# A transformer block on one core: VectorE takes row maxima ahead of a rotary tile, and the sums of modulation accumulators stand as a block behind a tile

## The chip, the core and the metric

The kernel runs on one core of a Trainium2 chip. The metric is the device time of one execution in microseconds. A core has five engines that run their own instruction streams and wait for each other on semaphores: TensorE (PE, matmuls), VectorE (DVE), ScalarE (ACT), GpSimd (POOL) and SyncE (SP, which here issues nearly all DMAs). Matmuls write to PSUM, eight banks of 128 x 512 float32.

## What is computed

One block of a hybrid network over 512 tokens of width 1024, in float32:

```
mod = silu(c) @ ada_w + ada_b
shift1, scale1, gate1, shift2, scale2, gate2 = split(mod, 6)
h = rmsnorm(x, norm1_w) * (1 + scale1) + shift1
gq, gk, gv, gr, g_lr, aq, ak, av, merge_a, merge_b = split(h @ w_in)
y_gla = (rmsnorm(gla_chunked(gq, gk, gv, log_sigmoid(g_lr @ w2 + b) / 16)) * silu(gr)) @ w_gla_branch
y_attn = dilated_attention(rotary(aq), rotary(ak), av) @ w_attn_branch
x = x + gate1 * ((sigmoid(merge_a) * y_gla + sigmoid(merge_b) * y_attn) @ w_out)
h2 = rmsnorm(x, norm2_w) * (1 + scale2) + shift2
x = x + gate2 * (causal_conv_ffn_hidden(h2, w_up, conv_w, conv_b) @ w_down)
out = rmsnorm(x, final_norm_w)
```

`dilated_attention` has three groups of four heads (dilations 1, 4, 16); each softmax needs the maximum of each row of scores. The `mod` vector is 6144 numbers, from a matrix of 25 MB.

## The kernel before

**Products.** Weights arrive in *units* of 1 MB or less (`UNITS`, line 90): ("v", ..), ("qk", p, g) for the query and key columns of head pair p and group g, ("lr", ..) for 16 columns of low rank, then ("gqk", h), ("gv", h), ("gr", h) for the four heads of the gated recurrence, and so on. Each unit gives one or two *tiles* (`tiles_of`), each 128 x 512 in PSUM. To keep float32 precision a weight is split into a high part (ScalarE, `split_hi`) and a rest (VectorE, `split_lo`), and so is h; a tile is 8 steps of k with 3 matmuls each (`three`, lines 1485 to 1487), 24 matmuls.

**Banks.** `TILES` lists all tiles in order; tile i lies in `bank[i % 2]`. `take(i)` (line 1515) waits on TensorE until the tile two places ahead has been read out and its bank is free (`acc_free`). Who reads it out depends on the kind: for "qk" VectorE in `rotate(j, t)` (L1054, L1055), j = 3p + g. The other six banks (`side`) are for attention and the recurrence.

**Modulation.** The last four parts of `mod` (gate1, shift2, scale2, gate2) are not made by TensorE alone. SP loads 16 chunks of 1 MB of `ada_w` between the units (`RAW`), two buffers taking turns. For each VectorE does `modulate(n)` (L1016 or L1018): multiply by a scalar per partition and add to `ada_acc`, 128 x 2048. After 8 chunks (r = 0 after n = 7, r = 1 after n = 15) TensorE sums over the partitions: 16 float32 matmuls of 128 columns of `ada_acc` against one column of ones (L1582), into the tile ("ada", r). VectorE adds the bias in `ada_tile(r)` (L1033), which frees that bank.

`WITH_ADA` names the two tiles that carry these sums: ("qk", 1, 2), 1 and ("gr", 2, 0), 1. In `TILES` the tile ("ada", r) stands ahead of the tile that carries it, and `product` puts three of the sums behind each k of that tile (`ada_part`).

**Attention for a pair of heads** (p = 0 beside the units ("qk", 1, g)) goes in steps `attention(p, i)`, written out on each engine: i = 0, 1 scores (TensorE), mask and maxima (VectorE); i = 2 TensorE transposes the maxima (L1662, L1664), VectorE takes the row maxima of both heads (L1109, L1111); i = 3 TensorE transposes them back (L1669, L1672), VectorE makes `negm` (L1116), ScalarE the exponentials (L643); i = 4 TensorE transposes (L1621), ScalarE and VectorE copy to PT (L656, L1125); i = 5, 6 the values. TensorE does a step between two tiles.

**Rotary.** `rotate` leaves products with cosine and sine in `rope` and `rope_t`; GpSimd adds the halves (L534) when both tiles of the unit are there. `rotate(j, 0)` waits for GpSimd to be through with j - 1 (`rope_sum`), as `rope_t` is used again. SP then issues eight shuffles to `qk` (L424) and the next weights; a load waits until its buffer has been used (`raw_used`, which VectorE counts up in `split_lo` and `modulate`).

The order on every engine is written out by hand: the engines' loops over p, g and t.

Of the kernel before, what the change touches and what calls it, by code (L numbers as in the profile page):

```python
# [19 lines left out]
KT = D // P  # L20
# [7 lines left out]
GROUPS = 3  # L28
# [80 lines left out]

WITH_ADA = {(("qk", 1, 2), 1): 0, (("gr", 2, 0), 1): 1}
TILES = []
for _u in UNITS:
    for _t in range(tiles_of(_u)):
        if (_u, _t) in WITH_ADA:
            TILES += [("ada", WITH_ADA[_u, _t])]
        TILES += [(_u, _t)]
    if _u == ("gqk", 0, 0):
        TILES += [("z", b) for b in range(NB)]  # L120
TILE = {t: n for n, t in enumerate(TILES)}
# [9 lines left out]
RAW_AT = {r: q for q, r in enumerate(RAW)}  # L131
# [19 lines left out]
def hybrid_block_kernel(nc, x, c, positions, ada_w, ada_b, norm1_w, w_in, gate_w2, gate_b, gla_norm_w,  # L151
# [3 lines left out]
    with ctx:  # L155
# [93 lines left out]
        bank = [ctx.enter_context(nc.psum_tensor(f"bank{i}", [P, SEQ], F32)) for i in range(8)]  # L249
# [4 lines left out]
        raw_used = sem("raw_used")  # L254
        hi_done = sem("hi_done")
        acc_ready = sem("acc_ready")
# [680 lines left out]
        def _(dve):  # L937
# [361 lines left out]
            for p in range(2):  # L1299
                for g in range(GROUPS):  # L1300
                    n = UNIT[("qk", p, g)]
                    if p == 0 or g == 0:
                        rotate(GROUPS * p + g, 0)
                        split_lo(n + 1)
                        rotate(GROUPS * p + g, 1)
                        modulate(n)
                        if p == 1:
                            attention(0, 0)
                    else:
                        split_lo(n + 1)  # L1310
                        if g == 1:
                            attention(0, 1)
                            rotate(GROUPS + g, 0)
                            modulate(n)
                        else:
                            rotate(GROUPS + g, 0)
                            attention(0, 3)
                            ada_tile(0)
                        rotate(GROUPS + g, 1)
                        if g == 2:  # L1320
                            modulate(n)
                        attention(0, 2 * g)
            n = UNIT[("lr", 0, 0)]
            split_lo(n + 1)
            modulate(n)
# [2 lines left out]
            for h in range(HEADS):  # L1328
                for u, kind in enumerate(("gqk", "gv", "gr")):
                    n = UNIT[(kind, h, 0)]  # L1330
# [24 lines left out]
            for u in range(4):  # L1355
                split_lo(UNIT[("ma", u, 0)] + 1)
                for t in range(2):
                    i = 2 * u + t
# [120 lines left out]
        def _(pe):  # L1479
# [35 lines left out]
            def take(i):  # L1515

                if i >= 2:
                    pe.wait_ge(acc_free[i % 2], i // 2)
                return bank[i % 2]

            def product(n, t):

                kind, a, _ = UNITS[n]
                slot = n % 2
                i = TILE[(UNITS[n], t)]
                ada = WITH_ADA.get((UNITS[n], t))
                if ada is not None:
                    take(i - 1)
                    pe.wait_ge(raw_used, RAW_AT[("ada", KT * (ada + 1) - 1)] + 1)
                dst = take(i)  # L1530
                if t == 0:
                    pe.wait_ge(raw_used, RAW_AT[("w", n)] + 1)
                if kind in ("v", "gv"):
                    for half in range(2):
                        blk = 2 * t + half
                        tok = slice(blk * P, (blk + 1) * P)
                        for k in range(KT):
                            w = tuple(v[:, slot, k * UW:(k + 1) * UW] for v in (w_hi, w_lo))
                            s = tuple(v[:, k, tok] for v in (h_hi, h_lo))
                            last = three(dst[:, half * UW:(half + 1) * UW], s, w, k == 0, k == KT - 1)  # L1540
                else:
                    if kind == "wa":
                        nk, width, at, src = 2, D, t * P, (oa_hi, oa_lo)
                    elif kind == "lr":
                        nk, width, at, src = KT, LOWRANK, 0, (h_hi, h_lo)
                    else:
                        nk, width, at = KT, UW, t * P
                        src = {"wg": (og_hi, og_lo), "wo": (mix_hi, mix_lo)}.get(kind, (h_hi, h_lo))
                    m = LOWRANK if kind == "lr" else P
                    if kind == "wa" and t == 0:  # L1550
                        pe.wait_ge(oalo_done, 2)
                    if kind == "wg" and a == 0 and t == 0:
                        pe.wait_ge(oglo_done, HEADS)
                    for k in range(nk):
                        if kind == "wo" and a == 0 and t == 0:
                            pe.wait_ge(mixlo_done, k + 1)
                        w = tuple(v[:, slot, k * width + at:k * width + at + m] for v in (w_hi, w_lo))
                        last = three(dst[0:m, :], w, tuple(v[:, k, :] for v in src), k == 0, k == nk - 1)
                        if ada is not None and k < nk - 1:
                            ada_part(ada, k)  # L1560
                last.then_inc(acc_ready, 1)

            def wide_values(half):
# [11 lines left out]
                if half == 0:  # L1575
                    last.then_inc(vw_half, 1)

            def ada_part(r, k):

                dst = bank[TILE[("ada", r)] % 2]  # L1580
                for j in range(3 * k, min(3 * k + 3, 2 * KT)):
                    last = pe.matmul(dst[:, j:j + 1], ada_acc[:, j * P:(j + 1) * P], ones[:, 0:1],  # L1582
                                     start=(j == 0), stop=True, skip_group_check=True)
                    if j == 2 * KT - 1:
                        last.then_inc(acc_ready, 1)

            def scores(hh, banks=range(4)):
                p, hd = divmod(hh, 2)
# [208 lines left out]
            for p in range(2):  # L1797
                for g in range(GROUPS):
                    for t in range(2):
                        product(UNIT[("qk", p, g)], t)  # L1800
                        if p == 1 and 2 * g + t > 0:
                            attention(0, 2 * g + t - 1)
            product(UNIT[("lr", 0, 0)], 0)
            attention(0, 5)

            for h in range(HEADS):
                for u, kind in enumerate(("gqk", "gv", "gr")):
                    for t in range(2):
                        i = 2 * u + t
                        product(UNIT[(kind, h, 0)], t)  # L1810
                        if h == 0 and i == 0:
                            attention(0, 6)
                        if h == 0:
                            attention(1, i)
                        if h == 1 and i == 0:
                            attention(1, 6)
                        if h >= 2 and i in (0, 2, 3):
                            gla(h - 2, 6 + i)
                        if h >= 1:
                            gla(h - 1, i)  # L1820
                    if h == 0 and kind == "gqk":
                        gate_tiles()

# [142 lines left out]
```

## Time and profile before

| | |
|---|---|
| median of 3 runs | 983.17 us (982.35 to 984.64) |
| profiled execution | 981.5 us, span of its core 979.7 us |
| TensorE busy, share of the span | 95% |
| VectorE | 53% |
| ScalarE | 38% |
| GpSimd | 10% |
| mean granted TensorE clock | 0.97 of full speed |
| read from HBM, written | 104.77 MB, 4.19 MB |
| chain of work that ended last: TensorE's share | 87% |

The span is the time from the first to the last instruction of the profiled execution. Matmul rows of the timeline carry a start and a duration; matmuls are pipelined, so durations overlap and the time that a run of them takes is read from start to start. The profiler records each float32 matmul of the sums as two (32 records for 16 matmuls). "Clock 1.00" in these rows is 2.4 GHz, 0.50 is 1.2 GHz.

### The profile page before, as it was taken

What the parts mean: (1) busy time and instruction counts of PE and PEld (TensorE: products, weight loads), DVE (VectorE), ACT (ScalarE), POOL (GpSimd) and SP (SyncE); (2) the same over time, 40 slices, a digit from 0 to 9 for tenths busy, and PEclk for the clock granted to TensorE, in tenths of its full rate; (3) what the DMA queues carried; (4) which work ended last, traced back from release to release, by engine and by line L of the source; (5) the groups of instructions that cost most, each with busy time, mean ns of one, the idle gap of its engine ahead of it and who ended that gap; (6) DMA issues with size and microseconds to landing.
All of it is one profiled execution on the core that took longest, in us unless ns stands there. A gap on an engine that the chain in (4) does not pass through costs nothing.

```text
span 979.7 us, 11999 instructions
## 1 busy us (share of the span) xinstructions
PE 931.3 (95%) x4659; PEld 782.5 (80%) x4659; DVE 522.8 (53%) x643; ACT 373.0 (38%) x457; POOL 94.6 (10%) x66
## 2 busy tenths in 40 slices
PE   2689998999999999999999997999999999999996
PEld 2589887779988988888888885888888888888885
DVE  5994774565574646463254436655555555523323
ACT  5362111547634334544322323433433344332225
POOL 4720421100000000000002222000000000000003
PEclk8699997989999999999999999999999999999998
DMA  9926764424351212122222441234333432322302
GB/s 323 355 90 190 213 186 121 151 87 140 118 173 50 80 43 87 45 85 86 86 87 86 172 129 54 75 98 116 86 86 100 114 86 86 114 102 86 120 9 86
DMA packets 114015, 112.68 MB, mean 115 GB/s; under 512 B 4516, under 2 KB 104230, under 8 KB 111671
## 3 DMA queue, kind: packets, MB, share of 16 engines
q1 hardware_dynamic: 113255, 109.96, 35.6%
q10 hardware_dynamic: 720, 2.16, 0.6%
q8 instruction: 28, 0.46, 0.2%
q14 instruction: 12, 0.10, 0.0%
HBM read 104.77 MB, written 4.19 MB: 111 GB/s over the span
## 4 chain that ended last, share of the span: by engine, by line
PE 87%; DVE 7%; issue 2%; DMA 1%; POOL 1%; SPq 1%; ACT 1%; DVEq 0%; ACTq 0%; POOLq 0%
PE bank L1485 25%; PE bank L1486 25%; PE bank L1487 25%; DVE ada_in L959 2%; PE bank L1700 2%; POOL rope L534 1%; DMA ada_in<-in_ada_w_dram 1%; PE bank L1582 1%; PE bank L1879 1%; PE bank L1721 1%; PE bank L1646 1%; DVE w_lo L993 1%; PE bank L1621 1%; DVE h_lo L1413 1%; DVE rope_t L1055 1%
## 5 line engine op out<-in xcount | busy, mean ns | idle before, releaser
L1485 PE MATMUL bank<-h_hi,w_hi 128*128 128x512 f32 (+1 forms) x696 | 278.7, 400 | 3.6 <-DVE rope_t L1055 2.6
L1487 PE MATMUL bank<-h_hi,w_lo 128*128 128x512 f32 (+1 forms) x696 | 273.0, 392 | 0.0
L1486 PE MATMUL bank<-h_lo,w_hi 128*128 128x512 f32 (+1 forms) x696 | 272.9, 392 | 0.0
L1485 PEld LDWEIGHTS bank<-h_hi,w_hi 128*128 128x128 f32 (+1 forms) x696 | 131.2, 188 | 32.2 <-issue 3.5
L1487 PEld LDWEIGHTS bank<-h_hi,w_lo 128*128 128x128 f32 (+1 forms) x696 | 131.0, 188 | 28.9
L1486 PEld LDWEIGHTS bank<-h_lo,w_hi 128*128 128x128 f32 (+1 forms) x696 | 131.2, 189 | 26.9 <-issue 0.2
L993 DVE TENSOR_TENSOR w_lo<-raw,w_hi 128x2048 fp32r<-128x2048 f32 (+3 forms) x48 | 88.2, 1848 | 61.8 <-ACT w_hi L566 61.8
L1000 DVE TENSOR_TENSOR w_lo<-raw,w_hi 128x2048 fp32r<-128x2048 f32 x32 | 73.4, 2293 | 88.8 <-ACT w_hi L574 88.8
L566 ACT ACTIVATE w_hi<-raw 128x2048 fp32r<-128x2048 f32 (+2 forms) x45 | 73.4, 1644 | 73.1 <-DMA raw<-in_w_in_dram 64.5
L1439 DVE SCALAR_TENSOR_TENSOR conv<-bank,vecs,conv 128x511 f32<-128x511 f32 x88 | 65.7, 748 | 66.5 <-ACT conv L888 61.0
L574 ACT ACTIVATE w_hi<-raw 128x2048 fp32r<-128x2048 f32 x33 | 62.9, 1905 | 69.3 <-PE bank L1487 69.3
L888 ACT ACTIVATE conv<-bank,vecs 128x512 f32<-128x512 f32 x44 | 34.1, 778 | 105.6 <-PE bank L1487 105.0
L1485 PE MATMUL bank<-hs_hi,w_hi 128*128 128x512 f32 x176 | 68.6, 390 | 0.0
L1487 PE MATMUL bank<-hs_hi,w_lo 128*128 128x512 f32 x176 | 68.5, 389 | 0.0
L1486 PE MATMUL bank<-hs_lo,w_hi 128*128 128x512 f32 x176 | 68.5, 389 | 0.0
L1485 PE MATMUL bank<-w_hi,h_hi 128*128 128x256 f32 (+1 forms) x160 | 50.5, 316 | 0.0
L1486 PE MATMUL bank<-w_lo,h_hi 128*128 128x256 f32 (+1 forms) x160 | 49.8, 311 | 0.0
L1487 PE MATMUL bank<-w_hi,h_lo 128*128 128x256 f32 (+1 forms) x160 | 49.8, 311 | 0.0
L1487 PEld LDWEIGHTS bank<-hs_hi,w_lo 128*128 128x128 f32 x176 | 33.0, 188 | 6.9
L1486 PEld LDWEIGHTS bank<-hs_lo,w_hi 128*128 128x128 f32 x176 | 33.0, 188 | 6.9
L1485 PEld LDWEIGHTS bank<-hs_hi,w_hi 128*128 128x128 f32 x176 | 33.0, 188 | 6.7
L506 POOL COPY sq_sum<-sq 128x512 f32<-128x512 f32 x3 | 1.8, 610 | 366.9 <-ACT sq L581 366.9
(235 smaller groups left out, 1340.1 us busy)
## 6 DMA issues: line engine op xcount, KB each, us to landing
raw<-in_w_up_dram SPq DMA_DIRECT2D x44, 512.0 KB, 4.5
raw<-in_w_in_dram SPq DMA_DIRECT2D x19, 1024.0 KB, 5.2
raw<-in_ada_w_dram SPq DMA_DIRECT2D x16, 1024.0 KB, 5.5
raw<-in_w_down_dram SPq DMA_DIRECT2D x22, 512.0 KB, 3.9
raw<-in_w_in_dram SPq DMA_DIRECT2D x20, 512.0 KB, 5.1
ada_in<-in_ada_w_dram SPq DMA_DIRECT2D x16, 512.0 KB, 8.9
raw<-in_w_gla_branch_dram SPq DMA_DIRECT2D x4, 1024.0 KB, 5.0
raw<-in_w_out_dram SPq DMA_DIRECT2D x4, 1024.0 KB, 5.3
```

What stands on the lines that cost most here:

```text
L534: pool.tensor_tensor(dst, dst, rope_t[:, half, :], op).then_inc(rope_sum, 1)
L566: last = act.activation(hv, r, ACT.Copy)
L574: act.activation(w_hi[:, slot, :], raw[:, slot, :], ACT.Copy).then_inc(hi_done, 1)
L888: act.activation(conv[:, s, t, :], bank[2 * s + t][:, :], ACT.Identity, scale=vecs[:, bass.ds(i + (V_CW2 + t * FT), 1)], bias=vecs[:, bass ...
L959: dve.scalar_tensor_tensor(total, ada_rows(j, k), c_silu[:, k:k + 1], total, ALU.mult, ALU.add).then_inc(ada_step, 1)
L993: last = dve.tensor_tensor(lv, r, hv.bitcast(F32), ALU.subtract)
L1000: dve.tensor_tensor(w_lo[:, slot, :], raw[:, slot, :], w_hi[:, slot, :].bitcast(F32), ALU.subtract).then_inc(raw_used, 1)
L1439: ins = dve.scalar_tensor_tensor(conv[:, s, t, tap:SEQ], src[:, 0:SEQ - tap], vecs[:, bass.ds(i + (col + t * FT), 1)], conv[:, s, t, tap:S ...
L1485: pe.matmul(out_ap, wh, xh, start=first, stop=False, skip_group_check=True)
L1486: pe.matmul(out_ap, wh, xl, start=False, stop=False, skip_group_check=True)
L1487: return pe.matmul(out_ap, wl, xh, start=False, stop=last, skip_group_check=True)
L1700: pe.matmul(side[2][0:m, at:at + CHUNK], kk[:, n, 0:m], q_in[:, h % 2, b * P + at:b * P + at + CHUNK], start=True, stop=True, skip_group_c ...
```

## The change

The table of tiles that carry sums becomes one of tiles that are followed by them; ("ada", r) moves behind its tile in `TILES`. TensorE no longer mixes the sums in: `modulation_sums(r)` issues all 16 in one block, the first after the tile ("qk", 1, 2), 1 and `attention(0, 4)`, ahead of ("lr", 0, 0); the second after ("gr", 2, 0), 1 and the recurrence's steps behind it, ahead of ("gqk", 3, 0). On VectorE the steps beside ("qk", 1, 1) and ("qk", 1, 2) stand in another order.

```diff
-WITH_ADA = {(("qk", 1, 2), 1): 0, (("gr", 2, 0), 1): 1}
+AFTER_TILE = {(("qk", 1, 2), 1): 0, (("gr", 2, 0), 1): 1}
 TILES = []
 for _u in UNITS:
     for _t in range(tiles_of(_u)):
-        if (_u, _t) in WITH_ADA:
-            TILES += [("ada", WITH_ADA[_u, _t])]
         TILES += [(_u, _t)]
+        if (_u, _t) in AFTER_TILE:
+            TILES += [("ada", AFTER_TILE[_u, _t])]
...
                         if p == 1:
                             attention(0, 0)
+                    elif g == 1:
+                        split_lo(n + 1)
+                        attention(0, 1)
+                        rotate(GROUPS + g, 0)
+                        attention(0, 2)
+                        rotate(GROUPS + g, 1)
+                        modulate(n)
                     else:
+                        rotate(GROUPS + g, 0)
+                        attention(0, 3)
                         split_lo(n + 1)
-                        if g == 1:
-                            attention(0, 1)
-                            rotate(GROUPS + g, 0)
-                            modulate(n)
-                        else:
-                            rotate(GROUPS + g, 0)
-                            attention(0, 3)
-                            ada_tile(0)
                         rotate(GROUPS + g, 1)
-                        if g == 2:
-                            modulate(n)
-                        attention(0, 2 * g)
+                        ada_tile(0)
+                        modulate(n)
+                        attention(0, 4)
...
                 i = TILE[(UNITS[n], t)]
-                ada = WITH_ADA.get((UNITS[n], t))
-                if ada is not None:
-                    take(i - 1)
-                    pe.wait_ge(raw_used, RAW_AT[("ada", KT * (ada + 1) - 1)] + 1)
                 dst = take(i)
...
                         last = three(dst[0:m, :], w, tuple(v[:, k, :] for v in src), k == 0, k == nk - 1)
-                        if ada is not None and k < nk - 1:
-                            ada_part(ada, k)
...
-            def ada_part(r, k):
-
-                dst = bank[TILE[("ada", r)] % 2]
-                for j in range(3 * k, min(3 * k + 3, 2 * KT)):
+            def modulation_sums(r):
+
+                dst = take(TILE[("ada", r)])
+                pe.wait_ge(raw_used, RAW_AT[("ada", KT * (r + 1) - 1)] + 1)
+                for j in range(2 * KT):
                     last = pe.matmul(dst[:, j:j + 1], ada_acc[:, j * P:(j + 1) * P], ones[:, 0:1],
                                      start=(j == 0), stop=True, skip_group_check=True)
-                    if j == 2 * KT - 1:
-                        last.then_inc(acc_ready, 1)
+                last.then_inc(acc_ready, 1)
...
+            modulation_sums(0)
             product(UNIT[("lr", 0, 0)], 0)
...
+                        if (kind, h, t) == ("gr", 2, 1):
+                            modulation_sums(1)
```

How this moves the instructions at two places. TensorE before, from the end of the tile ("qk", 1, 2), 0 (in `bank0`) on: the transposes of `attention(0, 3)`, then the next tile with its sums.

```order
L1487 MATMUL bank0<-h_hi,w_lo 128x512
L1669 MATMUL bank2<-cst,rowm 128x2 x4
L1672 MATMUL bank2<-cst,rowm 128x2 x4
L1485 MATMUL bank0<-h_hi,w_hi 128x512
L1486 MATMUL bank0<-h_lo,w_hi 128x512
L1487 MATMUL bank0<-h_hi,w_lo 128x512
L1582 MATMUL bank1<-ones,ada_acc 128x1 x3
L1485 MATMUL bank0<-h_hi,w_hi 128x512
```

TensorE with the change, at the same place:

```order
L1488 MATMUL bank0<-h_hi,w_lo 128x512
L1664 MATMUL bank2<-cst,rowm 128x2 x4
L1667 MATMUL bank2<-cst,rowm 128x2 x4
L1486 MATMUL bank1<-h_hi,w_hi 128x512
L1487 MATMUL bank1<-h_lo,w_hi 128x512
L1488 MATMUL bank1<-h_hi,w_lo 128x512
L1486 MATMUL bank1<-h_hi,w_hi 128x512
```

The tile is now in `bank1` and has no sums in it. TensorE with the change, from that tile's end on: the transposes of `attention(0, 4)`, the sums, the 16-column tile "lr".

```order
L1488 MATMUL bank1<-h_hi,w_lo 128x512
L1616 MATMUL bank2<-cst,S 128x128 x4
L1616 MATMUL bank3<-cst,S 128x128 x3
L1616 MATMUL bank4<-cst,S 128x128 x4
L1616 MATMUL bank5<-cst,S 128x128 x4
L1578 MATMUL bank0<-ones,ada_acc 128x1 x16
L1486 MATMUL bank1<-h_hi,w_hi 16x512
```

The sums stand in one row of 16, in `bank0`. VectorE beside ("qk", 1, 1), as a difference, from the end of `rotate(4, 0)` to `rotate(5, 0)` (L1054 and L1055 are a rotation, L1018 a part of the modulation, `rowm` the row maxima):

```order
 L1055 TENSOR_TENSOR rope_t<-bank0,cs 128x512
-L1018 SCALAR_TENSOR_TENSOR ada_acc<-raw,c_silu,ada_acc 128x2048
+L1109 COPY rowm<-bank2 2x512
+L1111 TENSOR_TENSOR rowm<-bank3,rowm 2x512
 L1054 TENSOR_TENSOR rope<-bank1,cs 128x512
 L1055 TENSOR_TENSOR rope_t<-bank1,cs 128x512
-L1109 COPY rowm<-bank2 2x512
-L1111 TENSOR_TENSOR rowm<-bank3,rowm 2x512
-L993 TENSOR_TENSOR w_lo<-raw,w_hi 128x128
+L1018 SCALAR_TENSOR_TENSOR ada_acc<-raw,c_silu,ada_acc 128x2048
 L1054 TENSOR_TENSOR rope<-bank0,cs 128x512
 L1055 TENSOR_TENSOR rope_t<-bank0,cs 128x512
```

The row maxima moved ahead of `rotate(4, 1)`, the modulation behind it. The same difference goes on, from `negm` to the first modulation part of r = 1:

```order
 L1116 TENSOR_SCALAR negm<-bank2 128x16
-L1033 TENSOR_TENSOR mod<-bank1,vecs 128x16
-L1054 TENSOR_TENSOR rope<-bank0,cs 128x512
-L1055 TENSOR_TENSOR rope_t<-bank0,cs 128x512
+L993 TENSOR_TENSOR w_lo<-raw,w_hi 128x128
+L1054 TENSOR_TENSOR rope<-bank1,cs 128x512
+L1055 TENSOR_TENSOR rope_t<-bank1,cs 128x512
+L1033 TENSOR_TENSOR mod<-bank0,vecs 128x16
 L1016 TENSOR_SCALAR ada_acc<-raw,c_silu 128x2048
```

`ada_tile(0)` (L1033) now stands behind `rotate(5, 1)`, and the small `split_lo` between the two rotations.

## Rows read from the trace of the kernel before

**Rows 1.** The page, part 2: granted clock of TensorE in 40 equal slices, in tenths.
```profile
PEclk8699997989999999999999999999999999999998
```

**Rows 2.** Stretches: length, each engine's busy time (x instructions), granted clock, DMA, GB/s.
```profile
159.00:176.00 17.00, 17.00 (x56) 14.79 (x57) 0.17 (x1) 3.90 (x12) 0.00 (x0) 0.50 0.33 86
176.10:188.20 12.10, 12.10 (x84) 8.87 (x83) 9.16 (x8) 8.07 (x19) 3.92 (x3) 1.00 0.43 132
213.70:220.30 6.60, 6.60 (x22) 4.50 (x21) 0.00 (x0) 5.22 (x11) 0.00 (x0) 0.50 0.00 0
336.00:344.00 8.00, 8.00 (x54) 7.14 (x52) 2.51 (x10) 1.02 (x1) 0.00 (x0) 1.00 0.34 117
599.20:602.60 3.40, 0.38 (x2) 0.37 (x3) 1.91 (x3) 2.35 (x5) 0.00 (x0) 1.00 0.00 0
602.70:606.00 3.30, 3.30 (x9) 2.56 (x9) 3.09 (x5) 3.17 (x4) 1.32 (x1) 0.50 0.01 2
607.70:610.20 2.50, 0.01 (x1) 0.00 (x0) 2.50 (x1) 0.00 (x0) 1.95 (x1) 1.00 0.00 0
```

**Rows 3.** TensorE's timeline, 148 to 189 us: start, duration, instructions [idle before, releaser].
```profile
148.77 0.60 PE L1662 MATMUL bank<-cst,mx 128*2 128x128 f32 x4
...
159.00 0.77 PE L1485 MATMUL bank<-h_hi,w_hi 128*128 128x512 f32 x1 [2.48 <-DVE rope_t L1055]
...
176.14 1.80 PE L1621 MATMUL bank<-cst,S 128*128 128x128 f32 x15
...
188.24 0.48 PE L1485 MATMUL bank<-h_hi,w_hi 128*128 128x512 f32 x1
```

**Rows 4.** VectorE's timeline, 149 to 181 us.
```profile
149.83 2.35 DVE L1018 SCALAR_TENSOR_TENSOR ada_acc<-raw,c_silu,ada_acc 128x2048 f32<-128x2048 f32 x1
152.09 1.05 DVE L1054 TENSOR_TENSOR rope<-bank,cs 128x512 f32<-128x512 f32 x1
...
154.02 0.67 DVE L1109 COPY rowm<-bank 2x512 f32<-2x512 f32 x1
...
156.85 1.05 DVE L1054 TENSOR_TENSOR rope<-bank,cs 128x512 f32<-128x512 f32 x1 [1.16 <-POOL rope L534]
...
178.36 1.27 DVE L1016 TENSOR_SCALAR ada_acc<-raw,c_silu 128x2048 f32<-128x2048 f32 x1
179.55 1.28 DVE L1125 COPY PT<-bank 128x512 f32<-128x512 f32 x2
```

**Rows 5.** GpSimd's timeline at 154 us.
```profile
154.25 2.56 POOL L534 TENSOR_TENSOR rope<-rope,rope_t 128x512 f32<-128x512 f32 x2 [18.29 <-DVE rope_t L1055]
```

**Rows 6.** ScalarE's timeline: exponentials of the first head; later, split of (gqk, 0, 0).
```profile
158.97 3.93 ACT L643 ACTIVATE S<-S,negm 128x256 f32<-128x256 f32 x12 [7.91 <-DVE negm L1116]
...
181.48 1.90 ACT L566 ACTIVATE w_hi<-raw 128x2048 fp32r<-128x2048 f32 x1
```

**Rows 7.** SP's timeline: the first chunk of r = 1, and the weights of (gqk, 0, 0).
```profile
152.21 0.35 SPq L389 DMA_DIRECT2D raw<-in_ada_w_dram  x1
...
162.48 0.58 SPq L398 DMA_DIRECT2D raw<-in_w_in_dram  x1
```

**Rows 8.** Chain that ended last: start, time on the chain, three sums at either clock.
```profile
160.62 1.07 PE bank L1582 x6
...
337.12 0.56 PE bank L1582 x6
```

**Rows 9.** TensorE's timeline, 327 to 350 us, around the tile (gr, 2, 0), 1.
```profile
327.67 0.58 PE L1485 MATMUL bank<-h_hi,w_hi 128*128 128x512 f32 x1
...
333.43 1.52 PE L1700 MATMUL bank<-q_in,kk 128*32 128x16 f32 x16
...
336.09 0.58 PE L1485 MATMUL bank<-h_hi,w_hi 128*128 128x512 f32 x1
...
345.52 1.52 PE L1700 MATMUL bank<-q_in,kk 128*32 128x16 f32 x16
...
349.19 0.50 PE L1485 MATMUL bank<-h_hi,w_hi 128*128 128x512 f32 x1 [0.66 <-DVE mod L1033]
```

## The prediction

> **What bounds the kernel now.** Begin with the page. TensorE is the engine that is busy nearly always, so a kernel like this gets shorter in two ways: TensorE waits less, or it works less time at the half clock. The line of the granted clock reads 9 or 10 tenths except in a few slices; the seventh of the 40 (147 to 171 us) shows 7 [rows 1]. The second view is the table of stretches: from 159.0 to 176.0 us TensorE is busy throughout at clock 0.50 (1.2 GHz), and from 176.1 on it is at 1.00 (2.4 GHz) [rows 2].
>
> TensorE's own timeline says what stands there [rows 3]. Before the tile (qk, 1, 2), 1 it idles 2.48 us, from 156.5 to 159.0, released by VectorE's L1055. This is the wait for the PSUM bank: tiles alternate between two banks, the accumulator tile "ada" 0 holds bank 1, so the tile needs bank 0, which `rotate(5, 0)` frees. VectorE's timeline shows that this rotation starts at 156.85, behind GpSimd, which adds the halves of the previous rotary pair until 154.25 + 2.56 = 156.81 and could begin only after VectorE's late rotation of that pair [rows 4, 5]. Then the tile, with the sums between its matmuls, takes 176.14 - 159.00 = 17.14 us. A tile of the same 24 matmuls alone takes 333.43 - 327.67 = 5.76 us at the full clock [rows 9].
>
> What the engine did around the moves of its clock: it had transposed a few columns and then idled when the clock fell; while one-column matmuls stood between the 512-column ones the clock stayed at 0.50 for 17 us; with the plain matmuls that end the tile it came back. At 336 to 344 us the same mixture runs at clock 1.00 [rows 2]: it does not bring the clock down, but from 0.50 it has not brought it up.
>
> **The change, part by part.** (1) The tile moves to the other bank: it takes bank 1, freed by `rotate(4, 1)` at about 153.2 (below). TensorE is done with the step before at 156.5. The wait of **2.48 us** goes. What is late next there: the transposes behind the tile need ScalarE's exponentials, see (3).
>
> (2) The sums stand behind the tile instead of inside. Six passes (three fp32 matmuls) take 0.56 us at clock 1.00 and 1.07 us at 0.50 [rows 8]. The 16 matmuls are 32 passes: 32/6 x 0.56 = 2.99 us, or 5.7 at the half clock. No row has such a block; these two bound it, and I take 2.99, as the block follows dense work at full clock. First place: 17.14 - 5.76 - 2.99 = **8.39 us** less. Second place: 349.19 - 336.09 = 13.10 us now; then a tile alone, 5.76, the steps of the recurrence behind it, 349.19 - 0.66 - 345.52 = 3.01, and the block, 2.99. So **1.34 us** goes, in it the 0.66 us that the next tile waited for VectorE's `ada_tile(1)`, since the bank it takes is then another [rows 9].
> A pass at full clock is 93 ns by the row, and 178 ns at the half clock. By the Trainium skill (TensorE: Matmul & The Clock Gate, LDWEIGHTS) a weight load costs its columns over 1.2: an estimate of 107 ns a pass, 3.4 us a block, and a gain that is smaller by 0.9 us over both. The row here is shorter and follows the clock; it decides.
>
> (3) VectorE's order. Nothing is added; steps change places. `attention(0, 2)` (two instructions, 0.67 us for the first) now precedes `rotate(4, 1)`. Its input is TensorE's transposes, which begin at 148.77, 1.1 us before VectorE turns to it at 149.83 [rows 3]: a few tenths of wait at most. `rotate(4, 1)` starts about 151.3 instead of 152.09, and the 2.35 us of modulation go behind it, to 155.5. GpSimd's 2.56 us then end at 156.0, `rotate(5, 0)` starts there, 0.85 us sooner than now, and so do `negm` and the exponentials behind it, which now start at 158.97 and take 3.93 us [rows 4 to 6]. They would end near 162.1. The moved tile ends at 156.5 + 5.76 = 162.3, and the last exponentials are wanted about a microsecond into the transposes. So this order saves 0 by itself, as cover: without it the margin would be some 0.5 us.
> `ada_tile(0)` and what is behind it on VectorE (`modulate(8)` and two copies to PT, 178.36 to 180.83 in the trace, 2.5 us) wait for the block's end: 162.3 + 1.8 of transposes [rows 3] + 3.0 = 167.1. They are done by 169.6. TensorE wants PT after the "lr" tile, another 24 matmuls, at 172.9. Hidden with 3 us to spare.
> SP's queue: `modulate(7)` ends 3.3 us later, so the load behind it is issued at 155.5 instead of 152.21. The eight shuffles behind wait for GpSimd as before, a little earlier, and the weights of (gqk, 0, 0) follow near 161.6 instead of 162.48 [rows 7]. Their split on ScalarE starts at 181.48 with no idle before it [rows 6]: it waits for the engine, not for a landing. With the exponentials of the second head through near 168, both halves are split by about 172. TensorE reaches them at 188.24 - 2.48 - 8.39 = 177.4: hidden with 5 us to spare.
>
> **The sum.** 2.48 + 8.39 + 1.34 = 12.2 us, if the clock stays up. Against this stands the clock in the new blocks: 3.0 us of one-column matmuls resemble the idle stretches. Of these, 599.2 to 602.6 brought the clock down and 607.7 to 610.2 did not [rows 2]. Between these ends I take one fall over the two blocks, with the shortest low stretch of the trace, 3.3 us (602.7 to 606.0), which costs half of itself, 1.65. So 12.2 - 1.65 = 10.6 us.
> The sum is against the profiled execution, 981.5 us (span 979.7), which is 1.67 us under the median of the runs, 983.17. The stretch that goes is one whose length varies with when the clock returns, so some of these 1.67 us may go too; I take half. 983.17 - 0.8 - 10.6 = **971.8 us**.
>
> **Rivals.** (A) No fall at all: 971.8 - 1.65 = 970.2. For it: the mixture at 336 to 344 held the clock, and 2.5 us of nothing did. (B) Both blocks bring it down and for long, as the 6.6 us at 213.7 to 220.3 [rows 2]: 3.3 us each, 970.2 + 6.6 = 976.8. For it: the first block follows 1.8 us of transposes, and if those are quiet too it is 4.8 us.
> The Trainium skill (the same page, Part 4: PE-mode transpose) says that transposes do not count as busy work for the clock. By it case B gains at the first block; no row here tests it alone.
> (C) The weights' chain does not come along: if they were split only when they are now, ScalarE's 181.48 plus some 4 us for both halves, TensorE would stand from 177.4 to 185.7, 8.3 us, and the time is 980.1. Against it: that queue was held by VectorE's waits, which end early. (D) **Slower**: the clock falls in each block and stays down for 17 us behind it, as it did from 159.0. Each costs half of 17.14, so 970.2 + 17.1 = 987.3. It decides whether the plain tiles behind a block bring the clock back; in the trace the end of the tile did. For no gain at all the low stretches must reach 25 us in total.
>
> **How the numbers follow.** Forecast 0.42, A 0.36, B 0.13, C 0.06, D 0.03. The forecast, A, B and half of C are faster by over 0.2% (2 us, about what a measurement of this kernel can tell): 0.94. The other half of C is within: 0.03. D is slower: 0.03. The range goes from A with all of the 1.67 us gone, and half of the low stretch at 213.7 with it (983.17 - 1.67 - 12.2 - 1.65 = 967.7), to B with nothing of the 0.8, 977.6; C and D stay out.
>
> **What would show it.** Right: no idle time before the tile at 156.5; clock 1.00 from 157 to 163; the 32 passes in one stretch of about 3.0 us from 164; the first tile of (gqk, 0, 0) near 177 instead of 188.24; (gqk, 3, 0) another 1.3 us earlier. For the forecast, one low stretch of 3 to 4 us that begins in or behind a block. Wrong: clock 0.50 for over 5 us behind a block; a new idle of TensorE for the exponentials at 162, for PT at 172 or for weights at 177; or a shift that is there at 177 and gone at 350.

## The result, and the profile after

| | before | changed |
|---|---|---|
| median | 983.12 us (8 runs, 982.35 to 984.64) | 977.32 us (8 runs, 972.8 to 980.22) |
| profiled execution, its span | 981.5, 979.7 us | 976.27, 974.5 us |
| mean clock of that execution | 0.970 | 0.969 |

The ratio is 0.9938, with a 95% interval of 0.9924 to 0.9953: the change gains 0.6%, 5.8 us, about half of what was forecast and 0.3 us inside the upper end of the range, less than the interval leaves open. Case B's number (976.8) lies close by. Two things catch the eye. The mean clock did not rise, although 17 us at half clock should have gone. And the runs spread over 7.4 us where before spread over 2.3; the fastest of the changed kernel had mean clock 0.975, those at 978.57 and 979.54 had 0.963, and the slowest, 980.22, had 0.965.

The granted clock, from the page of the changed kernel (part 2, against [rows 1]):

```profile
PEclk9589999979999999999999998999999999999998
```

The slice that read 7 (the seventh) now reads 9. The second is 5 instead of 6, the ninth 7 instead of 8, the 25th 8 instead of 9; the first and third are one higher. Stretches of the changed kernel, columns as in [rows 2]:

```profile
143.50:146.50 3.00, 3.00 (x9) 2.29 (x9) 3.00 (x6) 0.00 (x0) 0.00 (x0) 0.50 0.18 44
158.00:163.60 5.60, 5.60 (x26) 4.60 (x26) 2.33 (x4) 1.54 (x5) 1.86 (x2) 1.00 0.71 236
166.60:170.00 3.40, 3.40 (x34) 3.40 (x32) 0.00 (x0) 3.40 (x12) 2.44 (x3) 1.00 1.09 295
170.80:174.00 3.20, 3.20 (x9) 1.15 (x8) 2.86 (x4) 1.91 (x1) 0.00 (x0) 0.50 0.42 77
204.50:214.50 10.00, 9.91 (x21) 5.20 (x22) 2.44 (x6) 6.50 (x13) 0.00 (x0) 0.51 0.00 0
336.00:343.00 7.00, 7.00 (x63) 6.50 (x61) 0.79 (x2) 3.96 (x4) 0.00 (x0) 1.00 0.01 2
597.50:600.50 3.00, 3.00 (x8) 2.35 (x8) 2.90 (x4) 2.19 (x3) 2.00 (x1) 0.50 0.00 0
604.50:607.50 3.00, 3.00 (x8) 2.32 (x8) 2.79 (x5) 1.44 (x2) 0.00 (x0) 0.51 0.87 251
```

The moved tile (158.0 to 163.6) runs at 1.00; behind the first block (170.8) the clock is low for 3.4 us, behind the second it is not. Other low stretches stand where the change touches nothing: at 143.5, a longer one at 204 to 215, and two near 600 instead of one. By the granted clock of the profiles, and leaving out the old tile, the places of the two blocks and the last 10 us of the span, the clock was low for 37.5 us in the profile of before and for 51.2 in this one. These 13.7 us and the 3.4 behind the first block replace the 17 us that went, so the mean clock stayed. TensorE's timeline, first and second place, against [rows 3, 9]:

```profile
158.05 0.51 PE L1486 MATMUL bank<-h_hi,w_hi 128*128 128x512 f32 x1
...
163.67 0.93 PE L1616 MATMUL bank<-cst,S 128*128 128x128 f32 x7
164.88 0.66 PE L1616 MATMUL bank<-cst,S 128*128 128x128 f32 x4 [0.29 <-ACT S L643]
166.05 0.66 PE L1616 MATMUL bank<-cst,S 128*128 128x128 f32 x4 [0.51 <-ACT S L643]
166.55 3.63 PE L1578 MATMUL bank<-ones,ada_acc 128*128 128x1 f32 x32
170.04 0.39 PE L1486 MATMUL bank<-h_hi,w_hi 128*16 128x512 f32 x1
...
182.04 0.48 PE L1486 MATMUL bank<-h_hi,w_hi 128*128 128x512 f32 x1
```

```profile
330.95 0.58 PE L1486 MATMUL bank<-h_hi,w_hi 128*128 128x512 f32 x1
...
339.54 3.63 PE L1578 MATMUL bank<-ones,ada_acc 128*128 128x1 f32 x32
343.03 0.48 PE L1486 MATMUL bank<-h_hi,w_hi 128*128 128x512 f32 x1
```

The wait for the bank is gone, and the tile takes 163.67 - 158.05 = 5.62 us. But the transposes now take 166.55 - 163.67 = 2.88 us, with 0.8 us of idle time for ScalarE's exponentials, and a block takes 3.49 us, not 2.99. From the end of the step before (156.5 and 158.05) to the first tile of (gqk, 0, 0) it was 31.7 us and is 24.0: 7.7 less. The second place takes 343.03 - 330.95 = 12.08 instead of 13.10, 1.0 less. Those 8.7 us stand against 5.2 us of span. The other 3.5 were lost outside the two places, where the instructions are the same: 1.55 us ahead of the first place (158.05 against 156.5), 1.06 between the two (from 182.04 to 330.95, against 188.24 to 336.09) and 0.96 behind the second. In each of these parts the changed kernel's profile has more low clock than that of before.

Why the exponentials are late is on VectorE and GpSimd (against [rows 4, 5]). VectorE's timeline, then GpSimd's:

```profile
155.14 2.33 DVE L1018 SCALAR_TENSOR_TENSOR ada_acc<-raw,c_silu,ada_acc 128x2048 f32<-128x2048 f32 x1
159.89 1.08 DVE L1054 TENSOR_TENSOR rope<-bank,cs 128x512 f32<-128x512 f32 x1 [2.42 <-POOL rope L534]
```

```profile
155.35 4.51 POOL L534 TENSOR_TENSOR rope<-rope,rope_t 128x512 f32<-128x512 f32 x2 [19.16 <-DVE rope_t L1055]
```

GpSimd's two additions took 2.56 us in [rows 5] and take 4.51 now: the modulation part, 2.33 us on VectorE, has come to stand beside the first of them. The trace of before shows the same at another place, GpSimd's and VectorE's rows of the units ("qk", 0, g):

```profile
120.75 4.51 POOL L534 TENSOR_TENSOR rope<-rope,rope_t 128x512 f32<-128x512 f32 x2 [6.45 <-DVE rope_t L1055]
```

```profile
120.53 2.34 DVE L1018 SCALAR_TENSOR_TENSOR ada_acc<-raw,c_silu,ada_acc 128x2048 f32<-128x2048 f32 x1
```

The two additions are not slowed alike. L534 in the trace of before, ns min/median/max, from 120 and from 154 us:

```profile
L534 POOL TENSOR_TENSOR rope<-rope,rope_t x2: 1282/2276/3271, 120.8 to 124.0; 128x512 f32<-128x512 f32 x2
L534 POOL TENSOR_TENSOR rope<-rope,rope_t x2: 1292/1300/1309, 154.3 to 155.5; 128x512 f32<-128x512 f32 x2
```

The addition beside the modulation part takes 3.27 us, the one behind it 1.28 as ever. It loses nearly all of the time that it shares with VectorE's instruction.

So three questions: what the parts do alone, whether the blocks bring the clock down, and whether the low stretches elsewhere are the change's.

### The profile page after: what moved, and what is told of

Its sections match the earlier page's. It is cut to its first block, busy times and chain, and to the rows that moved or that the text cites. A ratio compares the mean times of both kernels' runs of the same rounds, so it can differ in the third digit from the quotient of the medians.

```text
span 974.5 us, 11999 instructions
## 1 busy us (share of the span) xinstructions
PE 929.3 (95%) x4659; PEld 780.5 (80%) x4659; DVE 522.8 (54%) x643; ACT 373.1 (38%) x457; POOL 95.8 (10%) x66
## 4 chain that ended last, share of the span: by engine, by line
PE 87%; DVE 6%; DMA 2%; issue 1%; POOL 1%; ACT 1%; SPq 1%; DVEq 0%; POOLq 0%; ACTq 0%
PE bank L1486 25%; PE bank L1488 25%; PE bank L1487 25%; DVE ada_in L959 2%; PE bank L1695 2%; POOL rope L534 1%; PE bank L1877 1%; DMA ada_in<-in_ada_w_dram 1%; PE bank L1641 1%; PE bank L1716 1%; PE bank L1682 1%; PE bank L1578 1%; DVE w_lo L993 1%; DVE h_lo L1414 1%; DMA raw<-in_w_in_dram 1%
```

## The experiments

Each diff is against the kernel named; a ratio is to runs of the kernel before on the same chip, with its 95% interval.

### The two kernels again, and each part alone

`before_again` and `after_again` are the two kernels unchanged.

> The kernel before, unchanged, to see in a second execution where its clock is low and what TensorE's wait ahead of the tile (qk, 1, 2), 1 takes up. Theory 1 (that wait is a cushion: it ends at a time that VectorE and GpSimd set, so whatever TensorE loses between 60 and 156 us is absorbed): the runs differ in their mean clock, but lie within about 2.5 us, around 983; if a low stretch stands ahead of 156 us, the wait is shorter than 2.48 us by about what it cost. Theory 2 (the runs of before have the same clock from run to run, and only the changed kernel's don't): the mean clocks agree to 0.001 and the wait is 2.5 us again. Rival for the time: drift between chips, over 984.7 or under 982.

> The changed kernel, unchanged. In its first profile TensorE's low stretches outside the place of the change add up to 52 us against 38 us before (each costs half): a stretch of 3.4 at 143, 3.4 more at 204 to 215, 3.4 more near 600, 3.4 more before 60. Theory 1 (these come and go from run to run and nothing takes them up now): the place of the change gives the same picture (block of 3.5 us, GpSimd's additions 4.5 us, TensorE idle 0.8 us for exponentials), but the low stretches stand elsewhere; runs spread over 6 to 8 us, and go with the mean clock at about 0.4 us for a us of low clock; median 976 to 978. Theory 2 (the blocks cause them all): a low stretch right behind both blocks in every profile, and the same total.

`sums_only` is the changed kernel with VectorE in the old order (`ada_tile(0)` behind `rotate(5, 1)`, as it must be). VectorE's part against the kernel before:

```diff
                     else:
                         split_lo(n + 1)
                         if g == 1:
                             attention(0, 1)
                             rotate(GROUPS + g, 0)
                             modulate(n)
                         else:
                             rotate(GROUPS + g, 0)
                             attention(0, 3)
-                            ada_tile(0)
                         rotate(GROUPS + g, 1)
                         if g == 2:
+                            ada_tile(0)
                             modulate(n)
                         attention(0, 2 * g)
```

> Only the sums moved behind their tiles; VectorE's steps beside (qk, 1, 1) in the old order, modulation ahead of rotate(4, 1), row maxima behind it. Theory 1 (GpSimd's additions take 4.5 us instead of 2.6 when VectorE's 2.3 us modulation runs beside them, so the new order made the exponentials later): GpSimd's L534 at about 154 us takes 2.6 us, negm stands at 158.8 (if no low stretch is ahead), TensorE's idle time in the transposes of S is under 0.3 us, and the time is about 1 us under the whole change: 975 to 977. Rival (the order moved negm ahead as predicted, so it is cover): 0.5 to 1 us over the whole change, with more idle at the transposes.

`order_only` is the kernel before with VectorE's new order; `ada_tile(0)` stays ahead of `rotate(GROUPS + g, 1)`:

> Only VectorE's order (row maxima ahead, modulation behind rotate(4, 1)); the sums stay mixed into the tiles, and TensorE again waits for rotate(5, 0). Theory 1 (GpSimd slowed by the modulation beside it): L534 takes 4.5 us, rotate(5, 0) starts near 158 instead of 156.85, the wait ahead of the tile grows by about 1 us to 3.5, and the time is 1 us longer than before: 984. Rival (the prediction's reckoning, additions 2.6 us): rotate(5, 0) near 156.0, the wait 1.6 us, 982.3.

| | median, us | ratio | interval |
|---|---|---|---|
| before_again | 982.89 | 0.9993 | 0.9980 to 1.0006 |
| after_again | 977.48 | 0.9936 | 0.9919 to 0.9953 |
| sums_only | 976.59 | 0.9931 | 0.9915 to 0.9948 |
| order_only | 983.60 | 1.0003 | 0.9991 to 1.0014 |

TensorE's timeline of before_again, then of order_only, at the wait ahead of the tile:

```profile
161.05 0.47 PE L1485 MATMUL bank<-h_hi,w_hi 128*128 128x512 f32 x1 [2.49 <-DVE rope_t L1055]
```

```profile
160.31 0.61 PE L1486 MATMUL bank<-h_hi,w_hi 128*128 128x512 f32 x1 [3.49 <-DVE rope_t L1055]
```

GpSimd's timeline of order_only, then of sums_only:

```profile
153.66 4.47 POOL L534 TENSOR_TENSOR rope<-rope,rope_t 128x512 f32<-128x512 f32 x2 [17.04 <-DVE rope_t L1055]
```

```profile
154.70 2.56 POOL L534 TENSOR_TENSOR rope<-rope,rope_t 128x512 f32<-128x512 f32 x2 [18.00 <-DVE rope_t L1055]
```

The order alone does what the theory of the slowed GpSimd says: 4.47 us of additions, and a wait that grows from 2.48 to 3.49. In the time this is +0.3 us, not to be told from nothing. With the old order the additions take 2.56 again, and TensorE's transposes stand in one piece:

```profile
162.52 1.80 PE L1615 MATMUL bank<-cst,S 128*128 128x128 f32 x15
164.16 3.63 PE L1577 MATMUL bank<-ones,ada_acc 128*128 128x1 f32 x32
```

1.64 us instead of 2.88: the 1.2 us that the new order loses are there in the trace, and the times (0.9931 and 0.9936) don't resolve them. All of the gain comes with the sums.

The cushion theory fell. In before_again the tile starts 2 us later than in the first profile, and the wait is 2.49 us all the same: what VectorE and GpSimd do there hangs on TensorE's tiles, so the whole chain moves. The other theory of that run asked for equal mean clocks, and they go from 0.963 to 0.971. The kernel before has a spread too, 980.25 to 985.70 in these 12 runs and 980.35 to 986.81 in the 23 that the ratios are taken to, so the 2.3 us of the first eight was a small sample. That low stretches elsewhere come and go with neither kernel's doing is what the profiles suggest: the one at 143 is absent in after_again, and that at 205 to 220 lasts 6.8 or 10.2 us in either kernel. Near 600 a second one stands in the changed kernel's two profiles, in neither of before's, but also in order_only's. Added up as above, the low clock elsewhere is 37.5 and 51.2 us in the two profiles of before, 51.2 and 47.8 in the two of the changed kernel, and 41.0 to 58.0 in those of the nine other kernels of this section. So the first pair of profiles set the least of all against a high one. The stretch at 143 is in two of the nine profiles without the wait (6.8 us long in wide_late) and in none of the four with it; it stands ahead of everything that the change moves, and what brings it is open.

### Do the blocks bring the clock down?

`wide`, against the changed kernel, multiplies by the same column of ones 128 times, and later sums overwrite what lies right of their column:

```diff
-                    last = pe.matmul(dst[:, j:j + 1], ada_acc[:, j * P:(j + 1) * P], ones[:, 0:1],
-                                     start=(j == 0), stop=True, skip_group_check=True)
+                    last = pe.matmul(dst[:, j:j + P], ada_acc[:, j * P:(j + 1) * P], ones[:, :],
+                                     start=True, stop=True, skip_group_check=True)
```

> The changed kernel, but each of the 32 sums multiplies against 128 columns of ones instead of one (the same column 128 times; a later sum overwrites what lies to the right). Theory 1 (a pass of the sums is bound by its weight load, 109 ns in the block, so 128 columns are free; and what brings the clock down is that one column leaves the array empty): the block takes 3.5 to 3.7 us, no low stretch of clock begins in or right behind either block, about 3.4 us of low clock at the first and 1 to 3 at the second fall away, and the time is 2 to 3 us under the whole change: 974.5 to 975.5. Theory 2 (the clock falls for another reason, the idle time at the transposes ahead of it): the block costs the same and the low stretch is still there; 977. Theory 3 (128 columns take longer than the load): the block takes over 6 us, and the time is over 980.

`mod_late`, against the changed kernel, puts the modulation part behind `negm`:

```diff
                         attention(0, 2)
                         rotate(GROUPS + g, 1)
-                        modulate(n)
                     else:
                         rotate(GROUPS + g, 0)
                         attention(0, 3)
+                        modulate(n - 1)
                         split_lo(n + 1)
```

> The changed kernel with the modulation part moved on behind negm (it stood behind rotate(4, 1), beside GpSimd's additions). Theory 1 (the modulation slows GpSimd from 2.6 to 4.5 us): L534 takes 2.6 us, rotate(5, 0) and negm stand 1.9 us sooner, TensorE's 0.8 us of idle time at the transposes of S go and the transposes take 1.6 us from first to last instead of 2.9; 1 to 1.3 us under the whole change: 976. Rival: the next chunk's load and the shuffles behind it in SP's queue are issued 3 to 5 us later, so TensorE waits for the weights of (gqk, 0, 0); over 977.4.

`next_tile` mixes the sums in again, but into the tile that follows. It is the kernel before with the changed kernel's order of VectorE and

```diff
-WITH_ADA = {(("qk", 1, 2), 1): 0, (("gr", 2, 0), 1): 1}
+WITH_ADA = {(("lr", 0, 0), 0): 0, (("gqk", 3, 0), 0): 1}
...
+                        attention(0, 4)
                         ada_tile(0)
                         modulate(n)
-                        attention(0, 4)
```

> The sums are mixed in again, three behind each k, but into the tile that follows (lr, and (gqk, 3, 0)), so that no tile waits for a bank; VectorE's order is that of the changed kernel, with the two copies to PT ahead of ada_tile(0). Theory 1 (a mixture does not bring the clock down, and only kept it low because it was low already from the wait): clock 1.00 or one low stretch at the first place, a mixed tile takes 9.4 us against 5.7 + 3.5 = 9.2 in a block, low clock at the two places falls to near 0, and the time is 1.5 to 3 us under the whole change: 974.5 to 976. Theory 2 (a mixture keeps a low clock low, and the idle time at the transposes brings it down first): clock 0.50 through the whole first mixed tile, 8 to 9 us of it, 4 us lost: 979 to 981.

`no_sums`, against the changed kernel, leaves out 15 of the 16 sums of either block, and so most of four of the six modulation vectors:

```diff
-                for j in range(2 * KT):
+                for j in range(1):
```

> The changed kernel with one sum instead of 16 in each block, so that 15 of 16 values of four of the six modulation vectors are not made: what the blocks cost. By their length, 2 x 15/16 x 3.5 = 6.5 us. Theory 1 (they also bring the clock down, 3.4 to 6.8 us of low clock in sum over both places, half of it lost): 8.5 to 10 us under the whole change, 967.5 to 969, and the low stretch behind the place of the first block is absent. Theory 2 (the clock's low stretch comes from the waits around, or from chance): 6.5 us under it, 971.

| | median, us | ratio | interval |
|---|---|---|---|
| wide | 973.37 | 0.9893 | 0.9875 to 0.9910 |
| mod_late | 975.37 | 0.9922 | 0.9903 to 0.9941 |
| next_tile | 973.88 | 0.9899 | 0.9881 to 0.9917 |
| no_sums | 965.80 | 0.9823 | 0.9807 to 0.9839 |

Wide against its one-column original: the block of wide in TensorE's timeline, and its stretches, from the block on at either place.

```profile
166.22 3.74 PE L1578 MATMUL bank<-ones,ada_acc 128*128 128x128 f32 x32
169.71 0.48 PE L1486 MATMUL bank<-h_hi,w_hi 128*16 128x512 f32 x1
```

```profile
166.30:170.00 3.70, 3.70 (x34) 3.58 (x33) 0.01 (x1) 3.70 (x13) 2.89 (x3) 1.00 0.98 269
170.00:175.30 5.30, 5.30 (x24) 2.27 (x23) 4.75 (x5) 2.21 (x3) 0.00 (x0) 1.00 0.56 167
337.80:347.00 9.20, 9.20 (x60) 8.24 (x59) 3.03 (x4) 1.16 (x1) 0.00 (x0) 1.00 0.20 61
```

128 columns cost no more than one: from the first sum to the next tile it is 169.71 - 166.22 = 3.49 us, as in the changed kernel. The clock stays at 1.00 at both places. 0.9893 against 0.9936 is 4.2 us; by the two intervals this difference is uncertain by some 2.4 us either way, an estimate. The idle time at the transposes (0.51 us, as in after_again, where the clock fell) is still there, so it alone does not bring the clock down. next_tile holds the clock as well: this mixture, entered at full clock, did not bring it down. Its first mixed tile:

```profile
166.63 0.40 PE L1486 MATMUL bank<-h_hi,w_hi 128*16 128x512 f32 x1
...
175.26 0.38 PE L1639 MATMUL bank<-PT,v_ext 128*128 128x128 f32 x2
```

That is 8.6 us at full clock for 24 matmuls and 16 sums. no_sums points the same way from the other side: 11.1 us under the whole change (0.9823 against 0.9936), where the length of the blocks explains 6.5. The other 4.6, uncertain by some 2.3, fit a clock that no longer falls there; low stretches elsewhere can have a part in them.

mod_late removes GpSimd's slow additions and TensorE's idle time. GpSimd's timeline, then TensorE's, then two stretches from the blocks on:

```profile
154.07 2.53 POOL L534 TENSOR_TENSOR rope<-rope,rope_t 128x512 f32<-128x512 f32 x2 [17.41 <-DVE rope_t L1055]
```

```profile
162.82 1.80 PE L1616 MATMUL bank<-cst,S 128*128 128x128 f32 x15
164.45 3.63 PE L1578 MATMUL bank<-ones,ada_acc 128*128 128x1 f32 x32
```

```profile
168.00:173.50 5.50, 5.50 (x25) 2.32 (x25) 2.57 (x4) 1.01 (x2) 0.21 (x1) 1.00 1.12 324
337.80:344.00 6.20, 6.20 (x19) 5.23 (x20) 2.54 (x3) 0.00 (x0) 0.00 (x0) 0.50 0.12 31
```

Here the first block passes with the clock up and the second brings it down. Over the profiles, low clock that begins in or right behind a block (from stretches of 1 us each):

| profile | first place | second place |
|---|---|---|
| changed kernel | 3.4 us | 0 |
| after_again | 6.8 | 0 |
| sums_only | 3.4 | 6.8 |
| mod_late | 0 | 6.8 |
| wide, wide_late, next_tile, next_late, no_sums | 0 | 0 |

In five of eight cases the clock fell in or right behind a one-column block, and in none of ten where the sums were wide, mixed or absent. Of the ten, four are wide blocks, so the times are needed beside the count.

What such a stretch costs can be read at one place, with the same instructions on TensorE. From the start of the moved tile to the first tile of (gqk, 0, 0), and in the block:

| profile | low clock | from tile to (gqk, 0, 0) |
|---|---|---|
| sums_only, mod_late | 3.4 us, 0 | 22.75 us, 21.20 us |
| after_again, wide | 6.8 us, 0 | 25.21 us, 22.08 us |

```profile
166.41 5.48 PE L1578 MATMUL bank<-ones,ada_acc 128*128 128x1 f32 x32
```

The first pair has no idle time at the transposes, the second 0.51 us each. 3.4 us of low clock cost 1.55 us and 6.8 cost 3.13, nearly half of themselves. The block of after_again (166.41), with the clock down in the midst of it, takes 171.75 - 166.41 = 5.34 us instead of 3.49. At the second place, from (gr, 2, 0), 1 to (gqk, 3, 0), sums_only and mod_late take 13.15 and 13.09 us: where the clock falls there, the gain on the 13.10 of before is gone.

### The kernel before with wide sums, and two combinations

`before_wide` is the same edit of the matmul in the kernel before; `wide_late` and `next_late` add mod_late's edit to wide and to next_tile.

> The kernel before, order and wait unchanged, with 128 columns of ones instead of one in the sums that are mixed into the two tiles. Theory 1 (the wait of 2.5 us brings the clock down, and the one-column matmuls keep it there): the wait and the fall at 159 to 162 stay, but the clock comes back after 3.4 to 6.8 us instead of 17, the mixed tile takes 11 to 13 us instead of 17.1, and the time is 4 to 6 us under before: 977 to 979. Theory 2 (the clock stays low as the mixture has pauses between its matmuls): 17 us low as before, 983.

> The changed kernel with both: 128 columns of ones in the blocks, and the modulation part behind negm. If the two causes are separate they add: no low clock at the two places, no idle time at the transposes, GpSimd's additions 2.6 us; 11.7 us under before, ratio 0.988, 971 to 972.5. If they are one cause, 0.989 to 0.990 as with either the wide sums or the mixture in the next tile alone.

> The sums mixed, one column each, into the tile that follows, and the modulation part behind negm. By the theory that a mixture does not bring the clock down: no low clock at the two places, the gain of the mixture (10.1 us against before) and the 1.3 us of the transposes add: 11.4 us, ratio 0.9885. Rival: with the idle time gone GpSimd's time is no longer on the path, but SP's shuffles go out later; TensorE waits, and nothing is added: 0.990.

| | median, us | ratio | interval |
|---|---|---|---|
| before_wide | 976.80 | 0.9935 | 0.9918 to 0.9952 |
| wide_late | 972.52 | 0.9889 | 0.9871 to 0.9908 |
| next_late | 973.30 | 0.9905 | 0.9888 to 0.9921 |

TensorE's timeline of before_wide, and its stretches in the mixed tile:

```profile
159.15 0.47 PE L1485 MATMUL bank<-h_hi,w_hi 128*128 128x512 f32 x1 [2.48 <-DVE rope_t L1055]
...
169.95 1.80 PE L1621 MATMUL bank<-cst,S 128*128 128x128 f32 x15
```

```profile
161.10:164.30 3.20, 3.20 (x13) 2.77 (x12) 0.00 (x0) 1.96 (x7) 0.00 (x0) 0.54 0.27 64
164.50:170.00 5.50, 5.50 (x36) 4.79 (x35) 0.17 (x1) 0.00 (x0) 0.00 (x0) 1.00 0.71 187
```

With no step moved, the same wait and the same fall, the tile takes 10.8 us instead of 17.1, because the clock is back after 3.4 us instead of 17. The time, 6.2 us less, is as good as that of the whole change. So the two causes stand apart. The one-column matmuls kept the clock down. What brought it down goes with the wait: it fell there in all four profiles that have the wait (with 0.9 us of two-column transposes ahead of it) and at that place in none of the nine that keep the transposes and lose the wait.

wide_late has the lowest ratio of the kernels that compute everything, its median 10.5 us under before; whether mod_late's edit adds to wide is open (0.9889 and 0.9893, intervals that overlap). At the first place it does: from the moved tile to (gqk, 0, 0) wide_late takes 21.30 us, wide 22.08. In next_late a new wait shows, on TensorE at the mixed tile, for the bank that `rotate(5, 1)` frees:

```profile
162.98 1.80 PE L1622 MATMUL bank<-cst,S 128*128 128x128 f32 x15
165.53 0.39 PE L1486 MATMUL bank<-h_hi,w_hi 128*16 128x512 f32 x1 [0.76 <-DVE rope_t L1055]
```

With a block behind the transposes that rotation is covered; here it is not. From the first transpose to the mixed tile it is 165.53 - 162.98 = 2.55 us, and 166.63 - 164.09 = 2.54 in next_tile, so at this place all that the later modulation part gained is given back. The rival in its expectation was right that nothing is added, but looked for the wait in SP's queue. The ratios, 0.9905 and 0.9899, do not tell the two kernels apart.

## Why the prediction came out as it did

**The wait for the bank (2.48 us): right.** It is gone, and nothing stands in its place at 156.5.

**The tile and sums at half clock (8.39 us): mechanism right, one price off.** The tile takes 5.62 us at clock 1.00. The block takes 3.49 instead of 2.99: the 0.56 us for six passes came from the chain, from sums that stand between wide matmuls, and the prediction took it for a block. In a block a pass takes 109 ns. Why it is shorter in the mixture was not tried. The price costs 0.5 us in either block, 1.0 us over both. The prediction had set its row above the 107 ns a pass that it estimated from the Trainium skill (TensorE: Matmul & The Clock Gate, LDWEIGHTS). The blocks of this case agree with that estimate, at 109 ns.

**The second place (1.34 us): right less that price,** 1.02 us in the profile of the changed kernel, where the clock stayed up.

**VectorE's order (0): wrong, 1.2 us.** The step "GpSimd's 2.56 us then end at 156.0" failed. The duration was read from a row in which VectorE did other work; the moved modulation part makes it 4.5 us, so rotate(5, 0) started 2.42 us after VectorE was free for it, and the exponentials came late instead of early. The price stood in the trace of before, at 120.75. `sums_only` and `mod_late` both take it away: the transposes take 1.64 and 1.63 us instead of 2.88. "A new idle of TensorE for the exponentials" was one of the signs of being wrong, and it came. That `ada_tile(0)` and SP's queue are covered held: PT and the weights were in time.

**The clock (1.65 us): right in kind, too small.** One fall with the shortest low stretch was taken. In the first profile of the changed kernel that is just what came, 3.4 us behind the first block. Over the four profiles with one-column blocks the mean is 6.8 us of low clock, some 3.2 us of time by the pairs above, an estimate. The times say 4.2 (wide) and 4.6 (no_sums), each uncertain by over 2. That lies between the forecast and rival B, which put two long falls at 6.6 us and had been given 0.13 against 0.42; no profile shows two long falls. The argument for B, quiet work by its width, should have weighed more, as the 17 us in the trace of before were a mixture with one-column work that did not bring the clock back. By the Trainium skill (TensorE: Matmul & The Clock Gate, Part 4: PE-mode transpose) the transposes ahead of a block add to it. No run decided that.

**The 0.8 us for a stretch that varies: no basis.** The low stretch of the old tile is 17 us in every profile that has it (two of before and order_only).

The sum with these: 12.2 - 1.0 - 1.2 - 4.2 = 5.8 us by the times of wide, or 6.8 with the 3.2 us of the profiles; measured 5.8. With terms this uncertain that the first hits the measured gain is luck. So is that the result lies at case B's number: the terms of the block and of VectorE's order, which B does not have, and the 0.8 us make up 3.0 of the 5.5 us from 971.8 to 977.3. What was right is the main part: the wait and the 17 us at half clock went. Not explained is why single executions of the changed kernel differ by up to 7 us. They go with the mean clock, and low stretches stand at different places from profile to profile; why they fall where they do was not tried.

## What to carry to other kernels

Price a moved instruction by a row in which it has the neighbours it will have: the same two GpSimd additions took 2.6 or 4.5 us, and both rows were there. One-column matmuls cost twice, by their length and by what they do to TensorE's clock: where 128 columns take no longer than one, as here, widen the moving side, or mix them with wide ones while the clock is up. If a stretch runs at half clock, ask separately what brought the clock down and what keeps it down; here the edit of one matmul against the second gave as much as removing the first. And add up the low clock outside the place of a change before reading two profiles against each other: here it differed by 13.7 us between two executions of the kernel before.

## What the runs showed of the hardware

- A float32 pass with one moving column took 109 ns in a block at clock 1.00, and one with 128 columns as long (3.49 us for 32, start to start, in the changed kernel and in wide).
- One-column matmuls for 3.5 us at clock 1.00 were followed, or overtaken before their end, by 3.4 or 6.8 us at 0.50 in five of eight cases; 128 columns in the same time in none of four. 3.4 us at 0.50 cost 1.55 us there. At 0.50 the clock stayed for 17 us under a mixture of 512 and one column, and came back after 3.4 us when the one was 128.
- GpSimd's tensor_tensor of 128x512 took 1.3 us, and 3.25 to 3.27 us where VectorE's 128x2048 scalar_tensor_tensor (2.33 us) ran beside it; the next one took 1.3 us again (2.53 to 2.57 us and 4.47 to 4.51 us for two).
